# Two-block transformer on one core: the index queries first in the core's filling, the second tile of the selection scored and selected inside the core, and another order between core and attention

## The chip, the cores and the metric

The kernel runs on one core of one Trainium2 chip. The time is device microseconds of one execution. A run of the comparison gives the median of several.

## What is computed

Two blocks work on 512 tokens of width 1024, in fp32. The first (gated linear attention, a convolution, attention in a window, a feed-forward net) is not touched. The second block has two layers. In each one, cut to what matters:

```python
h = rmsnorm_2(x, norm_mix[l]); proj = h @ w_in[l]
aq, ak, av, iq, ik, iw, hq, hf, hi, hg, ga, gb = jnp.split(proj, split_points, axis=-1)
aq, ak = rope(norm(aq)), rope(norm(ak))            # 8 heads of 64
iq, ik = rope(iq), rope(ik)                        # 4 index heads of 64, one key
# selection, per block of 128 queries
rel = relu(einsum('bqhd,bsd->bqhs', iq, ik)); score = einsum('bqh,bqhs->bqs', iw, rel)
_, idx = lax.top_k(where(visible, score, -inf), 128)
y_attn = softmax(q k_sel^T) v_sel
# HGRN core: S_t = diag(f_t) S_{t-1} + k_t v_t^T, o_t = S_t^T q_t, per head of 128
o = rmsnorm_2(o, hgrn_norm[l]) * silu(hg)
merged = sigmoid(ga) * (y_attn @ w_proj_attn[l]) + sigmoid(gb) * (o @ w_proj_hgrn[l])
x = x + merged @ w_out[l]                          # then the feed-forward net
```

The 128 largest scores of a query are found in 16 rounds, each of which takes the eight largest out of the row of scores. The first 128 queries see at most 128 keys and need no rounds, so three query tiles (m = 1, 2, 3, with 256, 384 and 512 scores a row) have 16 rounds each, 48 in a layer.

## The kernel before, in words

Each engine has its own program, written by hand in one order; they meet through semaphores. Every large product is fp32 by three products of split numbers: ScalarE rounds a weight panel (`wh`, line 925, in `ahead`), GpSimd subtracts the rounded part (`wl`, line 909, four pieces of 512 columns), TensorE multiplies (line 458). Weights come in panels of 1 MB in a ring of three slots; SyncE loads the next panel into a slot when the last product of its old panel is done (line 886), and `ahead` rounds it when ScalarE has passed far enough. Results lie in two PSUM pairs that TensorE fills in turn (`new_pair`) and ScalarE or VectorE must free.

A layer of the second block goes through these stages:

- **The core** (`core`, lines 534, 1039, 1508): 8 units, a unit being one tile of 128 tokens and two of the four heads. TensorE sums logarithms (559, 560), ScalarE takes exponentials (1051), VectorE multiplies seven levels of decays (1536), TensorE forms the pair products (580), VectorE copies them under masks (1540, 1550), TensorE makes output and state, VectorE reads both (1555, 1563). Since this is a chain with pauses, a second stream, **the filling** (`side_core_2`, lines 782, 1257, 1906), runs in fixed slots of each unit on all three engines. It has 40 steps, five a unit; on TensorE most are a quarter of a projection (12 matrix instructions of 512 columns, or 24 of 256). `core_steps` places them: one before the second sum, two before the pair products, one before the output, one at the unit's end. The filling projects the index key, the attention queries and keys, then the index queries, the values, and the first half of the output gate (`C_HG`).
- **Between core and attention** (`core_post`, lines 659, 1097, 1633): index scores of tiles 1 and 2 (`index`, `indexed`, `score_keys`), 28 of the 48 rounds (`select`, 1851 and 1853; the result, a bias, 1856), for each half j of the heads the sum of squares (668), the root by logarithm and exponential (1085 to 1095), the gate's arithmetic (`newton` 1628 and 1630, then 1643, 1647), rounding (1112) and the low part (1432). Eight steps of the merge of the first branch run beside it on TensorE.
- **Attention** (lines 673, 1126, 1654): 16 pairs of heads, four for each tile. Index scores of tile 3 come at its head; the remaining rounds and 16 more merge steps go between pairs.

Then the second merge, `w_out` and the feed-forward net follow, nearly all TensorE. For scoring, ScalarE rectifies the products into `tmp3` (line 1123) and VectorE weighs and adds them (1839, 1841); with one buffer, each rectification waits until the scores of the one before are read.

## Time and profile before

| what | us |
| --- | --- |
| median of 3 runs (2764.33 to 2767.23) | 2764.82 |
| the profiled execution's own time | 2762.72 |
| its span | 2760.9 |
| TensorE busy (share of the span) | 2613.3 (95%) |
| VectorE, ScalarE, GpSimd busy | 1161.3, 994.4, 1075.2 |
| core of the first layer, from to | 1037 to 1217.5 |
| between core and attention, from to | 1217.5 to 1279 |
| attention of the first layer, from to | 1279 to 1383 |

Times within the execution count from the span's start. TensorE is busy almost everywhere; the interest lies in the stretches where it is not.

### The profile page before, as it was taken

The numbers are of one execution on the slowest core, as the hardware profiler recorded it, in microseconds if no ns is written. First come the engines' busy times: TensorE is split into PE (matmuls) and PEld (weight loads), VectorE is DVE, ScalarE is ACT, GpSimd is POOL, SyncE is SP. The second block draws the span as 40 slices with busy tenths as digits, with TensorE's granted clock in tenths as the row PEclk, the third lists the DMA queues.
The fourth block names the chain that finished last, engine by engine and source line by source line (L and its number), as shares of the span: only waits on it lengthen the run. The fifth ranks groups of instructions, "written<-read, shape, count | busy, mean of one in ns | idle before, by whom it ended". The sixth has DMA issues, their size and how long they took to land.

```text
span 2760.9 us, 30113 instructions
## 1 busy us (share of the span) xinstructions
PE 2613.3 (95%) x12478; PEld 2125.0 (77%) x12478; DVE 1161.3 (42%) x1928; ACT 994.4 (36%) x1152; POOL 1075.2 (39%) x816
## 2 busy tenths in 40 slices
PE   6999999999999979997999999999998799999999
PEld 4887777887888767875687888888787568788887
DVE  5243343356423455758624211124575862511112
ACT  3423443343323344434424322234443442422220
POOL 3333332544445433212244544544321224354452
PEclk8999999999999999999999999999999899999999
DMA  4222212222232321111122322323111112232322
GB/s 146 68 77 76 77 62 77 92 92 92 92 106 88 96 71 52 46 46 61 31 92 92 105 94 92 107 92 92 46 47 47 61 42 94 88 99 92 102 96 76
DMA packets 206707, 221.05 MB, mean 80 GB/s; under 512 B 3713, under 2 KB 197467, under 8 KB 206443
## 3 DMA queue, kind: packets, MB, share of 16 engines
q1 hardware_dynamic: 206064, 218.97, 24.7%
q8 instruction: 99, 1.62, 0.2%
q14 instruction: 37, 0.30, 0.0%
q10 hardware_dynamic: 507, 0.15, 0.0%
HBM read 217.01 MB, written 2.10 MB: 79 GB/s over the span
## 4 chain that ended last, share of the span: by engine, by line
PE 82%; DVE 12%; ACT 5%; issue 1%; DMA 0%; DVEq 0%; SPq 0%; ACTq 0%
PE psum L458 72%; PE psum L580 2%; ACT wh L925 1%; DVE score L1853 1%; DVE top L1851 1%; PE psum L702 1%; PE psum L690 1%; PE psum L681 1%; DVE ul L1726 1%; DVE ul L1432 1%; DVE dec L1536 1%; PE psum L559 1%; DVE score L1841 1%; PE psum L560 1%; DVE merged L1749 1%
## 5 line engine op out<-in xcount | busy, mean ns | idle before, releaser
L909 POOL TENSOR_TENSOR wl<-raw,wh 128x512 fp32r<-128x512 f32 x812 | 1075.0, 1357 | 1659.8 <-ACT wh L925 1659.7
L458 PE MATMUL psum<-uh,wh 128*128 128x512 f32 x2024 | 812.4, 401 | 25.7 <-DVE ul L1726 4.4
L458 PE MATMUL psum<-ul,wh 128*128 128x512 f32 x2024 | 799.6, 395 | 0.0
L458 PE MATMUL psum<-uh,wl 128*128 128x512 f32 x2024 | 799.1, 395 | 0.0
L925 ACT CAST wh<-raw 128x2048 fp32r<-128x2048 f32 (+1 forms) x206 | 387.1, 1880 | 305.9 <-DMA raw<-in_w_ffn_out 118.0
L458 PEld LDWEIGHTS psum<-uh,wh 128*128 128x128 f32 x2024 | 387.8, 192 | 123.7 <-issue 22.0
L458 PEld LDWEIGHTS psum<-uh,wl 128*128 128x128 f32 x2024 | 386.4, 191 | 83.0
L458 PEld LDWEIGHTS psum<-ul,wh 128*128 128x128 f32 x2024 | 387.1, 191 | 79.2 <-issue 1.0
L458 PE MATMUL psum<-fh,wh 128*128 128x512 f32 x528 | 205.4, 389 | 0.0
L458 PE MATMUL psum<-fl,wh 128*128 128x512 f32 x528 | 205.4, 389 | 0.0
L458 PE MATMUL psum<-fh,wl 128*128 128x512 f32 x528 | 205.4, 389 | 0.0
L1768 DVE TENSOR_TENSOR xT<-xT,psum 128x1024 f32<-128x1024 f32 (+1 forms) x48 | 56.0, 1166 | 293.1 <-PE psum L458 292.8
L1814 DVE TENSOR_TENSOR tmp<-tmp,psum 128x1024 f32<-128x1024 f32 x22 | 26.9, 1221 | 357.5 <-PE psum L458 357.5
L458 PE MATMUL psum<-vh,wh 128*128 128x512 f32 x288 | 116.0, 403 | 10.2 <-DVE xT L1995 8.3
L458 PEld LDWEIGHTS psum<-fl,wh 128*128 128x128 f32 x528 | 99.1, 188 | 20.8
L458 PEld LDWEIGHTS psum<-fh,wl 128*128 128x128 f32 x528 | 99.1, 188 | 20.5
L458 PEld LDWEIGHTS psum<-fh,wh 128*128 128x128 f32 x528 | 99.1, 188 | 20.5
L458 PE MATMUL psum<-vh,wl 128*128 128x512 f32 x288 | 113.2, 393 | 0.0
L458 PE MATMUL psum<-wh,uh 128*128 128x256 f32 x320 | 94.2, 294 | 12.1 <-DVE ul L1432 12.1
L458 PE MATMUL psum<-vl,wh 128*128 128x512 f32 x256 | 99.7, 389 | 0.0
L458 PE MATMUL psum<-wl,uh 128*128 128x256 f32 x320 | 91.7, 286 | 0.0
L458 PE MATMUL psum<-wh,ul 128*128 128x256 f32 x320 | 91.6, 286 | 0.0
(318 smaller groups left out, 3276.1 us busy)
## 6 DMA issues: line engine op xcount, KB each, us to landing
raw<-in_w_in SPq DMA_DIRECT2D x78, 1024.0 KB, 5.2
raw<-in_w_ffn_in SPq DMA_DIRECT2D x44, 1024.0 KB, 5.1
raw<-in_w_up SPq DMA_DIRECT2D x22, 1024.0 KB, 5.1
raw<-in_w_ffn_out SPq DMA_DIRECT2D x16, 1024.0 KB, 5.1
raw<-in_w_down SPq DMA_DIRECT2D x8, 1024.0 KB, 5.0
raw<-in_w_out SPq DMA_DIRECT2D x8, 1024.0 KB, 5.1
raw<-in_w_ffn_out SPq DMA_DIRECT2D x8, 768.0 KB, 4.4
raw<-in_w_o SPq DMA_DIRECT2D x4, 1024.0 KB, 5.0
```

The source lines that it names most:

```text
L458: ins = mm(dst, x, y, start=first and i == 0, stop=last and i == len(todo) - 1)
L559: mm(X[1 + b][:, 0:3 * P], lth[:, u % 2, i, :], summask[:, cols], start=True, stop=False)
L560: ins = mm(X[1 + b][:, 0:3 * P], ltl[:, u % 2, i, :], summask[:, cols], start=False, stop=True)
L580: ins = mm(level_scores(l)[:, i, :, :], dec[:, i, l, :], odd_blocks(dec[:, i, l, :], l), start=True, stop=True)
L681: ins = mm(X[e][:, 0:(b1 - b0) * P], q[HD * e:HD * (e + 1), p, m * P:(m + 1) * P], kof(2 * p + e)[:, b0 * P:b1 * P], start=True, stop=True)
L690: ins = nc.tensor.transpose(X[2][:, b * P:(b + 1) * P], prob[i % 2][:, e, b * P:(b + 1) * P], ident)
L702: ins = mm(X[3][HD * e:HD * (e + 1), 0:P], vof(2 * p + e, b), probT[:, e, (b - b0) * P:(b - b0 + 1) * P], start=(b == b0), stop=(b == b1 - 1))
L909: ins = nc.gpsimd.tensor_tensor(wl[p % 3][:, w], raw[p % 3][:, w], wh[p % 3][:, w].bitcast(F32), ALU.subtract)
L925: nc.scalar.copy(wh[p % 3][:, 0:nk * width], raw[p % 3][:, 0:nk * width]).then_inc(S.hi_done, 1)
L1432: v.tensor_tensor(dst, src, high.bitcast(F32), ALU.subtract).then_inc(sem, 1)
L1536: ins = v.tensor_tensor(e[:, :, :, part, :], e[:, :, :, part, :], x[:, :, :, part, :], ALU.mult)
L1768: v.tensor_tensor(x, x, src, ALU.add).then_inc(pair_free[(n.q - 1) % 2], 1)
```

## The change

In words, for each of the two layers:

- The index queries (`C_IQ`) are projected second in the filling, before the attention queries; ScalarE and no longer VectorE copies them out and scales `iw`. The key's and queries' rotation comes in unit 1. The four norm-and-rotate groups of the attention queries and keys each move one unit later.
- Tile 1 is scored in unit 6 (step 31 of the filling, counted from 0), and its 16 rounds run inside the core: eight at the end of unit 6, eight at the end of unit 7.
- The second half of the output gate (`C_HG + 256`) is a panel of its own right behind the first, no longer between the merge's gates.
- Between core and attention stands `indexed_post`. The squares of the first half are taken before the core ends. Tile 2 is scored between the two halves of the gate, from two buffers (`rectified`), and nine of its rounds follow. Seven rounds of tile 2 and 16 of tile 3 are left for the attention (23, before 20). The merge steps stand two and six around the second sum, before four and four.
- TensorE goes on to the attention's first products when ScalarE has read the sums (`g_mean`), not when the root is done.
- `score1`, `bias1` and the second silu have places of their own, and tile 3 is rectified into two buffers.

The three `indexed_post` in the diff are TensorE's, ScalarE's and VectorE's, in this order; the piece with `index(1)` is from TensorE's filling, the last two pieces are from VectorE's.

```diff
-                  C_IK, C_AQ, C_AQ + 256, C_AK, C_AK + 256, C_IQ, C_AV, C_AV + 256, C_HG):
+                  C_IK, C_IQ, C_AQ, C_AQ + 256, C_AK, C_AK + 256, C_AV, C_AV + 256, C_HG, C_HG + 256):
...
-        merge(w, C_G2 + D, a["w_proj_hgrn_2"][l], C_HG + 256)
+        merge(w, C_G2 + D, a["w_proj_hgrn_2"][l])
...
-SIDE_POST_2 = (4, 4)
+SIDE_POST_2 = (2, 6)
...
-SELECT_EARLY = 14
+SELECT_CORE, SELECT_POST = (8, 8), 9
...
+            def indexed_post(side, side_steps):
+                sum_heads()
+                finish(project(uh, ul))
+                index(2)
+                take_on(side, side_steps[0])
+                sum_heads()
+                take_on(side, side_steps[1])
+                pe.wait_ge(S.g_mean, t.up(S.g_mean, 2))
...
                 yield from project_tokens()
-                pe.wait_ge(pair_free[queries % 2], queries // 2 + 1)
-                turn(iq, rot)
+                index(1)
                 yield
...
+            def indexed_post(side, side_steps):
+                root_heads()
                 act.wait_ge(S.i_scored, t.up(S.i_scored))
+                inverse_root(tmp[2][:]).then_inc(S.g_root, 1)
+                silu_gate(silu1[:])
+                rectify(2, 0)
+                high_branch(0)
+                rectify(2, 1)
+                act.wait_ge(S.out_read, t.up(S.out_read))
+                square_heads(1)
+                take_on(side, side_steps[0])
+                root_heads()
+                act.wait_ge(S.g_split, t.up(S.g_split))
+                inverse_root(tmp[2][:]).then_inc(S.g_root, 1)
+                take_on(side, side_steps[1] - 2)
+                high_branch(1)
+                take_on(side, 2)
...
+            def rectify(m, j):
+                src = next_pair()
+                act.wait_ge(S.pair_full, n.q)
+                fn(index_tiles(m)[j], src[:, :, 0:(m + 1) * P], ACT.Relu).then_inc(pair_free[(n.q - 1) % 2], 1)
+                ahead()
...
+            def indexed_post(g, side, side_steps, selection):
+                gate_heads(0, g, True, tmp[0][:])
+                next_pair()
+                score_keys(2)
+                take_on(selection, SELECT_POST)
+                take_on(side, side_steps[0])
+                gate_heads(1, g, True, silu1[:])
+                take_on(side, side_steps[1])
...
+                score_keys(1)
                 yield
                 yield from wait_steps(2)
-                cosine(iq[:])
+                take_on(selection, SELECT_CORE[0])
                 yield
                 yield from passed(1)
...
+                yield from wait_steps(3)
+                next_pair()
+                take_on(selection, SELECT_CORE[1])
                 yield
```

VectorE at the end of the core (line 1563 writes the last state) and behind it, in the kernel before; `score_80` and `score_81` are the scores of tiles 1 and 2:

```order
L1563 SCALAR_TENSOR_TENSOR state<-state,small,psum 128x128 x2
L2140 TENSOR_SCALAR hidden<-const 128x128
L1839 TENSOR_SCALAR score_80<-tmp,iw 128x256
L1841 SCALAR_TENSOR_TENSOR score_80<-tmp,iw,score_80 128x256 x3
L1844 TENSOR_TENSOR score_80<-score_80,const 128x128
L1839 TENSOR_SCALAR score_81<-tmp,iw 128x384
L1841 SCALAR_TENSOR_TENSOR score_81<-tmp,iw,score_81 128x384 x3
L1844 TENSOR_TENSOR score_81<-score_81,const 128x128
L1851 MAX top<-score_80 128x8
L1853 MATCH_REPLACE score_80<-top,score_80 128x256
...
L1628 TENSOR_TENSOR tmp<-tmp 128x1024
```

And now, from the scoring in unit 6 to the first product of the gate:

```order
L1897 TENSOR_SCALAR score_80<-tmp,iw 128x256
L1899 SCALAR_TENSOR_TENSOR score_80<-tmp,iw,score_80 128x256 x3
L1902 TENSOR_TENSOR score_80<-score_80,const 128x128
...
L1618 SCALAR_TENSOR_TENSOR state<-state,small,psum 128x128 x2
L1909 MAX top<-score_80 128x8
L1911 MATCH_REPLACE score_80<-top,score_80 128x256
...
L1579 COPY small<-dec 128x2
...
L1914 TENSOR_SCALAR bias_85<-score_80 128x256
L2205 TENSOR_SCALAR hidden<-const 128x128
L1683 TENSOR_TENSOR tmp<-tmp 128x1024
L1685 SCALAR_TENSOR_TENSOR tmp<-tmp 128x1024
```

Scoring and the first eight rounds stand in unit 6, ahead of the last unit's first operation (1579); the next eight and the bias behind the last state; nothing of tile 1 stands between core and gate any more.

ScalarE behind the core, in the kernel before (`tmp<-gq` is the square of the core's output, `early` a gate of the merge):

```order
L1300 ACTIVATE tmp<-psum 128x1024
L925 CAST wh<-raw 128x2048
L1123 ACTIVATE tmp<-psum 128x2x256 x2
L1123 ACTIVATE tmp<-psum 128x2x384 x2
L1101 ACTIVATE tmp<-gq 128x1024
L1085 ACTIVATE tmp<-psum,small 128x1024
L1088 ACT_TABLE_LOAD
L1088 ACTIVATE tmp<-tmp 128x1024
L1093 ACT_TABLE_LOAD
L1093 ACTIVATE tmp<-tmp 128x1024
L1095 ACTIVATE tmp<-tmp 128x1024
L1112 CAST brh_52<-tmp 128x1024
```

And now, from the first root's last operation on:

```order
L1114 ACTIVATE tmp<-tmp 128x1024
L1119 ACT_TABLE_LOAD
L1119 ACTIVATE silu_88<-psum 128x1024
L944 CAST wh<-raw 128x2048
L1147 ACTIVATE rectified_86<-psum 128x2x384
L944 CAST wh<-raw 128x2048
L1127 CAST brh_52<-tmp 128x1024
L1147 ACTIVATE rectified_87<-psum 128x2x384
L1123 ACTIVATE tmp<-gq 128x1024
```

The rounding of the first half (1127, before 1112) now stands behind the second silu and two weight panels (944).

## Rows read from the trace of the kernel before

**Rows 1.** Stretches: start:end, length; busy PE, PEld, DVE, ACT, POOL; clock, DMA share, GB/s.
```profile
1037.00:1217.50 180.50, 175.23 (x1015) 150.36 (x1015) 109.15 (x265) 73.79 (x73) 46.52 (x35) 0.98 0.16 47
1217.50:1279.00 61.50, 46.54 (x172) 33.14 (x172) 49.50 (x108) 32.82 (x30) 15.36 (x12) 0.85 0.22 69
1279.00:1383.00 104.00, 92.62 (x517) 63.94 (x517) 75.25 (x183) 43.46 (x106) 25.13 (x20) 0.92 0.12 37
2112.00:2173.50 61.50, 45.24 (x172) 32.75 (x172) 49.54 (x108) 32.81 (x30) 15.36 (x12) 0.88 0.22 69
```

**Rows 2.** The chain that ended last, cut to 1218 to 1383: shares by line.
```profile
by line: PE psum L458 24.2%; DVE score L1853 11.1%; DVE top L1851 10.1%; PE psum L702 6.4%; PE psum L690 6.1%; DVE score L1841 5.1%; PE psum L681 5.0%; ACT wh L925 3.2%; issue 3.0%; ACT tmp L1123 2.9%; DVE tmp L1643 1.7%; DVE score L1839 1.
```

**Rows 3.** ScalarE from the core's end: start, length, line, operation, idle before it.
```profile
1217.50 1.28 ACT L1300 ACT_TABLE_LOAD   x1 [10.09 <-PE psum L458]
...
1219.72 1.89 ACT L925 CAST wh<-raw 128x2048 fp32r<-128x2048 f32 x1
...
1238.30 1.12 ACT L1085 ACTIVATE tmp<-psum,small 128x1024 f32<-128x1024 f32 x1 [5.60 <-PE psum L668]
...
1244.20 1.06 ACT L1095 ACTIVATE tmp<-tmp 128x1024 f32<-128x1024 f32 x1
...
1276.50 1.04 ACT L1112 CAST brh<-tmp 128x1024 fp32r<-128x1024 f32 x1 [9.83 <-DVE tmp L1647]
```

**Rows 4.** VectorE, 1228 to 1272: scoring, rounds, the gate's first product.
```profile
1228.26 0.42 DVE L1839 TENSOR_SCALAR score<-tmp,iw 128x384 f32<-128x384 f32 x1 [0.62 <-ACT tmp L1123]
...
1230.34 1.27 DVE L1841 SCALAR_TENSOR_TENSOR score<-tmp,iw,score 128x384 f32<-128x384 f32 x2 [1.01 <-ACT tmp L1123]
...
1253.38 0.43 DVE L1851 MAX8 top<-score 128x8 f32<-128x256 f32 x1
...
1254.37 0.43 DVE L1851 MAX8 top<-score 128x8 f32<-128x256 f32 x1
...
1256.27 0.56 DVE L1851 MAX8 top<-score 128x8 f32<-128x384 f32 x1
...
1257.52 0.56 DVE L1851 MAX8 top<-score 128x8 f32<-128x384 f32 x1
...
1271.27 1.23 DVE L1628 TENSOR_TENSOR tmp<-tmp 128x1024 f32<-128x1024 f32 x1
```

**Rows 5.** GpSimd: the low parts of weight panels.
```profile
1065.71 10.48 POOL L909 TENSOR_TENSOR wl<-raw,wh 128x512 fp32r<-128x512 f32 x8 [13.22 <-ACT wh L925]
1099.62 5.01 POOL L909 TENSOR_TENSOR wl<-raw,wh 128x512 fp32r<-128x512 f32 x4 [23.42 <-ACT wh L925]
...
1254.81 10.09 POOL L909 TENSOR_TENSOR wl<-raw,wh 128x512 fp32r<-128x512 f32 x8 [27.79 <-ACT wh L925]
```

**Rows 6.** TensorE steps in the chain: start, length, line, matrix instructions.
```profile
1176.05 2.87 PE psum L458 x24
...
1214.69 2.75 PE psum L458 x12
...
1291.44 4.54 PE psum L458 x12
```

**Rows 7.** TensorE: one sum over the squares of two heads.
```profile
1236.38 1.88 PE L668 MATMUL psum<-tmp,ones 128*128 128x512 f32 x4
```

**Rows 8.** VectorE (two) and ScalarE (one) in the core's units 6 and 7.
```profile
1186.62 2.07 DVE L1970 TENSOR_TENSOR iq<-iq,tmp 128x1024 f32<-128x1024 f32 x1
...
1202.57 0.17 DVE L1524 COPY small<-dec 128x2 f32<-128x2 f32 x1 [8.45 <-ACT dec L1051]
...
1184.36 1.90 ACT L925 CAST wh<-raw 128x2048 fp32r<-128x2048 f32 x1 [2.95 <-DMA raw<-in_w_in]
```

**Rows 9.** VectorE: one level product of the core's unit 1 and one of unit 2.
```profile
1072.45 1.35 DVE L1536 TENSOR_TENSOR dec<-dec,gq 128x128 f32<-128x128 f32 x1
...
1099.29 0.29 DVE L1536 TENSOR_TENSOR dec<-dec,gq 128x128 f32<-128x128 f32 x1
```

**Rows 10.** ScalarE at the first pair of heads: the second rectification.
```profile
1286.11 1.03 ACT L1123 ACTIVATE tmp<-psum 128x1024 f32<-128x1024 f32 x1 [3.06 <-DVE score L1841]
```

More of the change, by code:

```diff
@@ L115, in __init__ @@
         self.pair_scaled = sem("pair_scaled")
+        self.g_mean = sem("g_mean")
         self.alpha_done = sem("alpha_done")
@@ L340, in build_program, with index_tiles @@
         gaT = at("gaT", 63, [RANK, T])
+        def index_tiles(m):
+            if m == 1:
+                return [tmp[3][:].rearrange("p a (b t) -> p (a b) t", b=2)[:, 2 * j:2 * j + 2, :] for j in range(2)]
+            return [(rectified[0] if m == 2 else tmp[3])[:, :, 0:(m + 1) * P], rectified[1][:, :, 0:(m + 1) * P]]
         sq = at("sq", 49, [P, MC, T])
@@ L359, in build_program @@
         inverse = at("inverse", 48.5, [P, P])
-        bias1 = at("bias1", 44, [P, 2 * P])
+        bias1 = nc.alloc_sbuf_tensor_at("bias1", [P, 2 * P], F32, offset=walpha_at + 4 * 2 * P)
+        rectified = [at(f"rectified{i}", 32 + 4 * i, [P, 2, T]) for i in range(2)]
+        silu1 = at("silu1", 12, [P, 2, T])
         bias2 = at("bias2", 42, [P, 3 * P])
@@ L784, in side_core_2 @@
                 yield from project(uh, ul, (0,))
-                keys = n.q - 1
+                yield from project(uh, ul)
+                queries = n.q - 1
+                dst = new_pair()
+                mm(dst[:, 0, :], rot, ik[:], start=True, stop=True)
+                for m in range(NT):
+                    ins = nc.tensor.transpose(dst[:, 1, 4 * m:4 * m + 4], iwT[:, m * P:(m + 1) * P], ident[HD:HD + 4, HD:HD + 4])
+                ins.then_inc(S.pair_full, 1)
+                pe.wait_ge(pair_free[queries % 2], queries // 2 + 1)
+                turn(iq, rot)
+                yield
                 for j in range(4):
@@ L796, in side_core_2 @@
                     yield
-                yield from project(uh, ul)
-                queries = n.q - 1
-                dst = new_pair()
-                pe.wait_ge(pair_free[keys % 2], keys // 2 + 1)
-                for m in range(NT):
-                    nc.tensor.transpose(dst[:, 1, 4 * m:4 * m + 4], iwT[:, m * P:(m + 1) * P], ident[HD:HD + 4, HD:HD + 4])
-                mm(dst[:, 0, :], rot, ik[:], start=True, stop=True).then_inc(S.pair_full, 1)
-                yield
                 yield from project_tokens()
-                pe.wait_ge(pair_free[queries % 2], queries // 2 + 1)
-                turn(iq, rot)
+                index(1)
                 yield
@@ L1279, in side_core_2 @@
                 yield from passed(2)
+                yield from evict(iq[:])
+                src = next_pair()
+                act.wait_ge(S.pair_full, n.q)
+                fn(tmp[1][:, 0, :], src[:, 0, :], ACT.Copy)
+                fn(iw[:].rearrange("p m h -> p (m h)"), src[:, 1, 0:4 * NT], ACT.Copy,
+                   scale=1.0 / 16).then_inc(pair_free[(n.q - 1) % 2], 1)
+                ahead()
+                next_pair()
+                ahead()
+                yield
                 for j in range(4):
@@ new lines, in gate_heads @@
+            def gate_heads(j, g, same, gate):
+                dve.wait_ge(S.g_root, t.up(S.g_root))
+                newton(tmp[1][:], tmp[2][:])
+                for i in range(2):
+                    col = g if same else g + 2 * j + i
+                    ins = v.scalar_tensor_tensor(tmp[3][:, i, :], gq[:, 2 * j + i, :], vech[:, col:col + 1],
+                                                 tmp[3][:, i, :], ALU.mult, ALU.mult)
+                ins.then_inc(S.dve_chain, 1)
+                dve.wait_ge(S.dve_chain, t.up(S.dve_chain))
+                v.tensor_tensor(tmp[3][:], tmp[3][:], gate, ALU.mult).then_inc(S.g_prod, 1)
+                dve.wait_ge(S.g_prod, t.up(S.g_prod))
+                dve.wait_ge(S.b_hi, t.up(S.b_hi))
+                low(brl[0][:, 2 * j:2 * j + 2, :], tmp[3][:], brh[0][:, 2 * j:2 * j + 2, :],
+                    S.branch_ready if j else S.g_split)
@@ L2137, in _ @@
                     dve.wait_ge(S.dve_chain, t.up(S.dve_chain))
-                core(1.0, side_core_2(l), SIDE_CORE_2)
+                selection = select_all()
+                core(1.0, side_core_2(l, selection), SIDE_CORE_2)
                 side = merge(early, first=True)
```

174 lines of the change are left out of this document (77 added, 97 removed).

## The prediction

> **What bounds it now.** The page says that TensorE is almost always busy, so a gain can only come out of its pauses. I looked for them with the table of stretches. The core of the first layer keeps TensorE busy for 175.2 of 180.5 us; between core and attention it is 46.5 of 61.5, part of that at a granted clock of 0.85, and in attention 92.6 of 104 [rows 1]. The second layer's stretch between core and attention is as long [rows 1], so every term below counts twice. The chain of waits, cut to the stage, says who sets the pace: besides TensorE's products its largest shares are VectorE's rounds (L1853, L1851), 21%, then scoring L1841 [rows 2]. Between core and attention VectorE is the bound: it is busy 49.5 of 61.5 us [rows 1] and nearly all the rest is a hand-over with ScalarE. At the end of the core it is the other way round: before unit 7 VectorE stands idle for 8.45 us [rows 8]. The change moves VectorE's work from the one place to the other.
>
> I count from t = 0 at 1217.5, where TensorE's last step of the core has ended [rows 6] and ScalarE starts the silu of the gate [rows 3]. The stage ends with the gate's product of the second half of the heads, for which ScalarE's rounding L1112 waits until 1276.50 [rows 3]: t = 59.0. From there on attention follows in nearly the same order before and after.
>
> **The new path from t = 0 to that product.** The durations are those of the rows.
>
> - ScalarE: table and silu, until the cast of a panel begins, 2.2; cast until 4.1; first root, from the start of L1085 to the end of L1095 7.0 [rows 3]. The squares were made before the core's end and TensorE's sum takes 1.9 [rows 7], which is hidden. The root is ready at 11.1. VectorE's product (from L1628's start to the waiting copy) takes 5.2 [rows 3, 4]: 16.3. VectorE's eight rounds behind the last state end near t = 6.5 and hold nobody.
> - TensorE: sum 1.9, then the second gate projection, four steps of 2.75 [rows 6]: 12.9. ScalarE: table and silu 2.2, cast 1.9: 17.0. It rectifies half of tile 2, 0.8 for 768 of the 1024 columns that take 1.03 [rows 10]: 17.8. Then a second cast is ahead of the rounding. Its panel may be loaded only from 12.9 on; in unit 6 a step ended at 1178.92 and the cast of the panel so released began at 1184.36 [rows 6, 8], 5.4 later. So: begin at 18.4, end at 20.3, rounding 1.0 [rows 3]: 21.3. VectorE, done at 16.3, waits five microseconds for this.
> - VectorE: low part 1.2, scoring of tile 2 0.42 + about 0.65 + 1.27 + 0.3 [rows 4], together 3.9. But GpSimd splits the two panels from 17 to 27 (5.0 a panel [rows 5]), and an instruction of VectorE with two SBUF inputs is held up when it starts in the middle of that: the same 1024 columns take 2.07 in L1970 and 1.23 in L1628 [rows 8, 4], a level product 1.35 against 0.29 [rows 9]. Four instructions at about 0.9 more: ready at 28.7. Nine rounds of 384 at 1.25 (the distance of two maxima [rows 4]): 40.0. I take the rounds as not held up, since those from 1256.27 on keep the distance while GpSimd works on the two panels that it began at 1254.81 [rows 4, 5]. The product of the second half, 5.2: **t = 45.2, a gain of 13.8**.
> - TensorE has in that time 1.9 + 11 + 8 steps of 2.75 + 1.9, near 38 us with index products, so it isn't the bound; the second root (7.0 from about 25) is ready before 40.
>
> **Inside the core.**
>
> - Unit 6, step 31. Removed are the rotation of the index queries: 1.23 and, held up by GpSimd, 2.07 [rows 8]. Added is the scoring of tile 1, 0.4 + 3 x 0.6 + 0.3, but its second half waits for a rectification that stands behind the cast at 1184.36 to 1186.3 [rows 8], and the three instructions then meet GpSimd. The masks begin near 1190.9 and no longer at 1188.7: **2.2 lost**. Bounds: 0 if nothing is held up, 5 if all seven of scoring's and rounding's instructions are.
> - The normalization that moves into unit 6 stood in four of the other units up to now, in a core that keeps TensorE busy for 175.2 of 180.5 us [rows 1]; I cost it at nothing, since the slot is the same and the exponential behind it comes as late there.
> - The eight rounds of 0.98 [rows 4] at the end of unit 6, 7.9, go into the idle 8.45 [rows 8]. I cost them at nothing; the cover is thin, 0.6 us, and anything beyond lengthens the core one for one. Bounds 0 and 7.9; I take the lower end because the idle row is the very place.
> - Unit 1: the index queries' rotation comes here. In unit 1 GpSimd splits two panels in one go, 10.5 us, and the level products start into it, at 1.35 each [rows 5, 9]. That stays, with ScalarE about 1 us earlier: **1.0 gained**. The copies that ScalarE takes over are as long as VectorE's and lie in its idle time.
>
> **Attention.** 23 rounds instead of 20 fall on 11 pairs, one more each at pairs 0, 5 and 10. At pair 0 VectorE is the bound: **1.25 lost**. At the other two the pace is nearly even: **0.8 lost** of 2.9 (bounds 0 and 2.9). The second rectification of tile 3 waited 3.06 us for its buffer [rows 10] and now has its own; VectorE gets back about **1.2**, the rectification's 1.03 and a hand-over.
>
> **Sum.** Per layer -13.8 + 2.2 - 1.0 + 1.25 + 0.8 - 1.2 = -11.75, for two layers -23.5. The profiled execution took 2762.7 ; it lies 2.1 below the median of 2764.8. So 2739.2 against the former, **2741** against the latter.
>
> The Trainium skill ("ScalarE: Activation LUTs", What ACT_TABLE_LOAD costs) states 2.66 us for each switch of tables, 1.28 of load and 1.38 of drain. By that, the path to 21.3 would be some 0.8 longer and the sum -22. The trace shows 1.28, and the cast 2.2 after the load's start leaves no room for a drain behind it [rows 3], so the sum goes by the trace.
>
> **The rivals.**
>
> 1. *VectorE is freed fully.* If ScalarE's second panel cast is early and GpSimd's pieces fall beside the scoring, the stage falls by about 17 and unit 6 loses nothing: -17.5 a layer, **2730**. For it: GpSimd's panels and VectorE's bursts often miss each other, as in unit 2 with 0.29 [rows 9]. Against it: both casts stand in the order right ahead of the rounding. Chance 0.15.
> 2. *TensorE's clock takes half.* The new path leaves TensorE pauses at t = 13 to 18 and 42 to 57. A step at the lower clock takes 4.54 and not 2.75 [rows 6], and in attention the clock is 0.92 now [rows 1]. Three or four more such steps where TensorE leads cost 6 a layer: **2753**. Chance 0.12.
> 3. *The rounds in the core are exposed.* Unit 6 is late by the scoring (3.5 beyond the 2.2) and the eight rounds then lie before the level products: 7.9. That eats the 11.75: **2765**, no change. Chance 0.06.
> 4. *Slower: collisions in units 2 to 5.* There the level products end just before GpSimd starts on its panel: the last of unit 2 at 1099.58, the panel at 1099.62 [rows 5, 9]. If the shifted projections let a panel start 3 to 4 us sooner than the products, each unit has four products waiting for a piece of GpSimd, near 1.05 each: 4.2. All four units in both layers give +33.6: **2775**. It decides against the change from the sixth unit hit of eight on. Against it: in these units the cast waits for the load of its panel, and that comes from the same step as now. Chance 0.05. The Trainium skill ("SBUF — State Buffer", SBUF: two separate sides) says that the port VectorE and GpSimd share is locked for a whole instruction and the loser waits; that is what the two lengths of a level product show here.
>
> **How the numbers follow.** My case has 0.62, with its own range from the bounds: 2735 (nothing held up in unit 6) to 2749 (5 in unit 6, 2.9 in attention, one more held-up chain). Rivals 1 and 2 are faster too. A measurement of this kernel tells about 0.2%, 5.5 us, from no change, that is below 2759 or above 2770. Faster 0.87 (the first three cases, less 0.02 for the end of rival 2's), within 0.2% 0.07, slower 0.06. The range, 2729 to 2757, takes in my case and most of rivals 1 and 2, and leaves out 3 and 4 and the tails.
>
> **What would show it.** Right: the core still ends within 2 or 3 us of where it did, counted from its start; the product of the second half comes 44 to 48 us after that; attention lasts 103 to 105; in the chain cut to the stage the rounds' share falls from 21% to about 15%; the rounding of the first half waits for nobody but comes behind two casts. Wrong: level products of 1.3 us in units 2 to 5 (rival 4), an idle VectorE before unit 7 gone and the unit longer (rival 3), steps of 4.5 us in attention (rival 2), a second product before t = 42 (rival 1). If the core changes its length outside units 1 and 6, the count is wrong there.

## The result, and the profile after

The changed kernel takes **2751.9 us** (median of four runs, 2748.07 to 2755.41), the kernel before 2765.4 on the same chip (four runs): a ratio of 0.995, 95% interval 0.9933 to 0.9967. In a later series it took 2749.2 (five runs, 2746.4 to 2750.38), ratio 0.9941 (0.9928 to 0.9953). All nine runs have a median of 2749.5; experiments are set against that number below, since the kernel before had medians of 2764.0 to 2764.3 in the three series of experiments. It is faster, by 13 to 15 us, and the forecast was 23.5. The profiled execution took 2752.76, its span is 2751.0 against 2760.9. 2751.9 lies inside the stated range of 2729 to 2757, but not in the range of the forecast's own case, 2735 to 2749, and nearer to rival 2's 2753 than to the 2741 of the sum: some 5 us a layer are missing, and below they are looked for term by term.

The page's first lines, and the table of stretches of the changed kernel. The stretches are the core of the first layer, the stage between core and attention, attention, and that stage in the second layer.

```profile
span 2751.0 us, 30103 instructions
PE 2609.2 (95%) x12478; PEld 2123.0 (77%) x12478; DVE 1175.1 (43%) x1924; ACT 996.1 (36%) x1158; POOL 1078.3 (39%) x816
```
```profile
1037.00:1224.00 187.00, 180.16 (x1021) 154.19 (x1020) 120.71 (x298) 78.86 (x81) 45.65 (x34) 0.95 0.15 46
1224.00:1271.00 47.00, 38.77 (x164) 28.91 (x162) 36.95 (x64) 28.83 (x26) 16.54 (x12) 0.98 0.29 90
1271.00:1376.60 105.60, 92.71 (x517) 62.78 (x517) 81.64 (x193) 43.24 (x106) 26.53 (x20) 0.93 0.12 36
2115.00:2162.50 47.50, 38.71 (x164) 28.92 (x162) 37.42 (x67) 29.33 (x26) 16.55 (x12) 0.98 0.28 89
```

Set against [rows 1]: the stage fell from 61.5 to 47.0, as forecast, but the core grew from 180.5 to 187.0 and attention from 104.0 to 105.6. The core's growth is not even over its eight units. The next table is worked out from VectorE's updates of the state, one at each unit's end (L1559 and L1563 before, L1614 and L1618 after); unit 0 is counted from VectorE's copy of the decay (L1524, L1579). "First attention" is the distance from the last state to VectorE's first masked logits.

```
us                     unit 0  unit 1  2 to 4 each  unit 5  unit 6  unit 7  first attention
before, layer 1         11.98   30.61        22.0    20.06   21.34   21.21     64.18
before, layer 2         12.00   30.51        22.1    20.08   21.33   21.22     64.18
after, layer 1          11.99   30.60        22.0    22.30   23.66   22.40     50.01
after, layer 2          15.65   30.47        22.1    22.29   23.55   22.34     50.01
after, second profile:
  layer 1               11.99   30.53        22.0    22.29   23.04   21.22     49.98
  layer 2               11.98   30.61        22.1    22.29   22.99   21.22     49.97
```

So a layer loses 2.2 in unit 5, 1.7 to 2.3 in unit 6, nothing or 1.2 in unit 7, and in unit 0 of one layer 3.65. It gains 14.2 behind the core and loses some 1.4 in attention. With a start 0.7 later, the first layer comes to -6.3 (from 1382.90 to 1376.58 at attention's end), the second to -3.6: together the 9.9 of the spans. The start itself says nothing about the change: the first layer's core begins at 1043.40 before and at 1044.11 after, and anywhere from 1043.1 to 1047.1 in the fourteen profiles of this document, with the same program ahead of it.

**Behind the core.** ScalarE, then VectorE; columns are start, length, engine, line, operation, and in brackets the idle time before it.

```profile
1236.56 1.03 ACT L1119 ACTIVATE silu<-psum 128x1024 f32<-128x1024 f32 x1 [1.66 <-PE psum L468]
1237.48 1.89 ACT L944 CAST wh<-raw 128x2048 fp32r<-128x2048 f32 x1
1239.27 0.81 ACT L1147 ACTIVATE rectified<-psum 128x768 f32<-128x768 f32 x1
1241.61 1.91 ACT L944 CAST wh<-raw 128x2048 fp32r<-128x2048 f32 x1 [1.53 <-DMA raw<-in_w_proj_hgrn]
1243.42 1.04 ACT L1127 CAST brh<-tmp 128x1024 fp32r<-128x1024 f32 x1
...
1268.78 1.04 ACT L1127 CAST brh<-tmp 128x1024 fp32r<-128x1024 f32 x1 [12.71 <-DVE tmp L1697]
```
```profile
1244.57 2.25 DVE L1487 TENSOR_TENSOR brl<-tmp,brh 128x1024 fp32r<-128x1024 f32 x1 [5.67 <-ACT brh L1127]
1246.85 1.30 DVE L1897 TENSOR_SCALAR score<-rectified,iw 128x384 f32<-128x384 f32 x1
1248.19 3.76 DVE L1899 SCALAR_TENSOR_TENSOR score<-rectified,iw,score 128x384 f32<-128x384 f32 x3
```
```profile
1239.44 11.44 POOL L928 TENSOR_TENSOR wl<-raw,wh 128x512 fp32r<-128x512 f32 x8 [7.53 <-ACT wh L944]
```

The sum is the forecast's nearly to the microsecond. The first half's rounding stands behind two casts and ends at 1244.4, t = 20.6 from the core's end at 1223.9 (forecast 21.3); VectorE idles 5.67 for it (forecast "five"); GpSimd's two panels cover low part and scoring, of which five instructions and not four are held up, by 3.7 us together where 3.6 were forecast (the additions take 1.25 each); the second half's product reaches ScalarE at 1268.78, t = 44.9 (forecast 45.2). The last row answers to the last of [rows 3]. One piece went another way: the forecast had a table load in front of each silu, and the trace has the second one made at 1233.62, before the 1.66 of idle shown above. The product of the first half was ready at t = 15.0 and not 16.3. This changed nothing, since the rounding hung on the second panel, whose cast began at 17.7 (forecast 18.4).

**In units 5 and 6.** TensorE before the change (unit 5), then after it (unit 5, and the row at which unit 6 waits):

```profile
1159.80 0.40 PE L802 MATMUL psum<-const,iwT 4*128 4x4 f32 x4
1160.14 1.12 PE L803 MATMUL psum<-ik,const 128*128 128x512 f32 x2
```
```profile
1160.53 1.96 PE L822 MATMUL psum<-qksq,const 128*128 128x512 f32 x4
1162.32 1.88 PE L800 MATMUL psum<-ak,const 128*128 128x512 f32 x4
...
1183.07 1.13 PE L752 MATMUL psum<-ik,iq 64*128 64x256 f32 x8
...
1196.79 0.49 PE L600 MATMUL psum<-attT,gv 128*128 128x128 f32 x2 [2.03 <-DVE attT L1605]
```

Unit 5 now holds the means and the rotation of the last normalization, 3.8 us of TensorE, where the index keys' small rotation with 1.5 stood. No run moves the normalization alone; that it costs the 2.2 is read from these rows (3.8 less 1.5, in a unit in which TensorE is busy throughout). In unit 6 TensorE waits 2.03 us for the masks, which VectorE copies behind the scoring of tile 1:

```profile
1188.69 0.48 DVE L1899 SCALAR_TENSOR_TENSOR score<-tmp,iw,score 128x256 f32<-128x256 f32 x1
1189.92 2.44 DVE L1899 SCALAR_TENSOR_TENSOR score<-tmp,iw,score 128x256 f32<-128x256 f32 x2 [0.75 <-ACT tmp L1147]
1192.39 1.27 DVE L1902 TENSOR_TENSOR score<-score,const 128x128 f32<-128x128 f32 x1
...
1194.17 2.56 DVE L1605 COPY_PREDICATED attT<-pairmask,psum 128x128 f32<-128x128 uint8 x7
...
1209.02 0.17 DVE L1579 COPY small<-dec 128x2 f32<-128x2 f32 x1 [1.77 <-ACT dec L1070]
```

The last row answers to the 8.45 of [rows 8]: with the eight rounds ahead of it VectorE still idles 1.77 before unit 7, and 0.58 in the second profile, whose unit 6 is shorter.

### The profile page after: what moved, and what is told of

The parts are those of the page before. It is cut to its first block, busy times and chain, and to the rows that moved or that the text cites. A ratio compares the mean times of both kernels' runs of the same rounds, so it can differ in the third digit from the quotient of the medians.

```text
span 2751.0 us, 30103 instructions
## 1 busy us (share of the span) xinstructions
PE 2609.2 (95%) x12478; PEld 2123.0 (77%) x12478; DVE 1175.1 (43%) x1924; ACT 996.1 (36%) x1158; POOL 1078.3 (39%) x816
## 4 chain that ended last, share of the span: by engine, by line
PE 80%; DVE 13%; ACT 4%; DMA 1%; issue 1%; DVEq 0%; SPq 0%; ACTq 0%
PE psum L468 71%; ACT wh L944 2%; PE psum L590 2%; DVE score L1911 1%; DVE top L1909 1%; DVE score L1899 1%; PE psum L723 1%; DVE ul L1790 1%; DVE dec L1591 1%; PE psum L711 1%; DVE ul L1487 1%; PE psum L569 1%; DVE tmp L1736 1%; DVE merged L1813 1%; DVE normed L1548 1%
## 5 line engine op out<-in xcount | busy, mean ns | idle before, releaser
L468 PEld LDWEIGHTS psum<-fh,wl 128*128 128x128 f32 x528 | 99.1, 188 | 20.6
L468 PEld LDWEIGHTS psum<-fh,wh 128*128 128x128 f32 x528 | 99.1, 188 | 20.6
```

The lines of the kernel that those rows point to most:

```text
L468: ins = mm(dst, x, y, start=first and i == 0, stop=last and i == len(todo) - 1)
```

## The experiments

In the diffs, `rectify(m, j, False)` and `silu_gate(dst, False)` leave out the `ahead()` behind the activation, that is, the cast of the next panel, which is made at the next `ahead()`. `ahead(done=1)` counts one more pair of results as finished, so that both panels that wait there are cast at once.

### 1. Casts away from the level products of units 0 and 1

```diff
@@ ScalarE, side_core_2, the changed kernel @@
-                yield from passed(2)
-                yield from evict(iq[:])
+                yield
+                next_pair()
+                yield
+                yield
+                ahead(done=1)
+                yield
+                yield
+                src = next_pair()
+                act.wait_ge(S.pair_full, n.q)
+                fn(iq[:], src, ACT.Copy).then_inc(pair_free[(n.q - 1) % 2], 1)
+                ahead()
+                yield
```

> On the changed kernel: ScalarE's two casts of panels that stand before the level products of units 0 and 1 are moved behind the copy of unit 0's transposed keys, so that GpSimd splits both of them beside the masks of unit 0; unit 1 then has one panel and not two. Nothing else is moved. Theory A (GpSimd's panels hold up VectorE's level products in unit 1, TensorE is bound there by it, and which of the two wins in unit 0 differs from layer to layer): level products of 0.29 in unit 0 of both layers and mostly in unit 1, unit 1 shorter by 5 to 8 us, unit 0 of the second layer by 3.6: 12 to 20 us in all, about 2736. Theory B (unit 1 is bound by TensorE's own products): less than 4 us gained.

The same in the kernel before the change, whose first group of projections is a normalization:

```diff
@@ ScalarE, side_core_2, the kernel before @@
-                yield from passed(2)
+                yield
+                next_pair()
+                yield
                 for j in range(4):
-                    yield from wait_steps(3)
+                    yield
+                    if j == 0:
+                        ahead(done=1)
+                    yield from wait_steps(2)
```

> The same displacement of casts in the kernel before the change, whose unit 1 still holds a normalization (its means and rotation are 3.6 us of TensorE). Theory A (the changed kernel lost 2.2 us in unit 5 to the normalization that came there, and got nothing back in unit 1 only since GpSimd binds that unit): unit 1 gets shorter here too, but stays 2 us longer than in the changed kernel with displaced casts, so that the two differ by 2 to 4 us more for two layers than before and after do, 15.5 to 17.5 instead of 13.5. Theory B (the place of the normalization is indifferent): they differ by 13.5 as before.

Measured: on the changed kernel **2727.5** (2724.03 to 2730.42; ratio to before 0.987, 0.9856 to 0.9883), 22 below the changed kernel; on the kernel before 2746.3 (ratio 0.9939, 0.9925 to 0.9952), 17.8 below it. Rows of the first of the two kernels, GpSimd and a level product of unit 1:

```profile
1053.80 10.01 POOL L928 TENSOR_TENSOR wl<-raw,wh 128x512 fp32r<-128x512 f32 x8 [10.61 <-ACT wh L944]
1072.66 4.99 POOL L928 TENSOR_TENSOR wl<-raw,wh 128x512 fp32r<-128x512 f32 x4 [8.85 <-ACT wh L944]
```
```profile
1068.87 0.29 DVE L1601 TENSOR_TENSOR dec<-dec,gq 128x128 f32<-128x128 f32 x1
```

No level product of any unit is held up in either kernel, and unit 1 takes 21.15 (changed) and 21.6 (before) where it took 30.6. Theory A holds, with more gained than it said: 9.4 us in each layer were the price of seven held-up products out of 16 and of what follows from the late levels. The kernel before had this loss too, and the change left it alone.

Not all of it is waiting. Behind the pair products TensorE has twelve instructions of a projection. Their stretch before the change, after it, and nearly the whole of unit 1 with the casts moved; the columns are those of [rows 1], the clock the third figure from the end, and the count takes in one instruction at each edge:

```profile
1080.90:1084.90 4.00, 4.00 (x14) 3.25 (x14) 1.38 (x4) 0.00 (x0) 0.00 (x0) 0.68 0.00 0
```
```profile
1080.65:1085.60 4.95, 4.95 (x14) 3.92 (x14) 1.39 (x4) 0.00 (x0) 0.00 (x0) 0.54 0.00 0
```
```profile
1054.00:1079.00 25.00, 25.00 (x138) 20.69 (x138) 11.56 (x37) 8.18 (x9) 14.80 (x12) 1.00 0.14 43
```

TensorE waits up to 1.9 us at a time for the late levels, and behind that it is granted the lower of its two levels (1.2 and not 2.4 GHz) for 6.9 us in the kernel before and for 10.2 in every unit 1 of the changed kernel. The twelve take 4.0 and 4.95 us; with the casts moved, at a clock of 1.00, they take 2.85. So of the 9.4 us 7.3 lie ahead of the end of the pair products and 2.1 are the clock behind them.

The second expectation failed in both its numbers. The two unit 1s differ by 0.45, not 2: what the normalization left behind in unit 1 was at once filled by the index queries' rotation (1.98, and 1.4 for the keys, against 3.8). And the medians of the two kernels differ by 18.8, more than the 15.5 to 17.5 of theory A and than theory B's 13.5; unit 1 accounts for 0.9 of that, and no run shows the rest. So the 2.2 of unit 5 is no exchange that a hidden stall swallowed: only 0.45 comes back in unit 1 and 0.3 in unit 6 (section 3).

### 2. Chance in unit 0

```diff
@@ ScalarE, side_core_2, against the first kernel of section 1 @@
-                ahead(done=1)
+                ahead()
```

With this only unit 0's panel moves. Beside it the changed kernel ran once more, unedited.

> The changed kernel itself once more, for the spread of its runs and a second profile. In the profiles so far the four last level products of unit 0 are either all held up by GpSimd (unit of 15.65 us) or none of them (12.0), in one of the two layers or in neither, with the same program around them. Theory A (this is left to chance in every run, and is the spread): single runs lie apart by up to 7.3 us, median between 2748 and 2754. Theory B (it is set by the program): all runs within 3 us.

> On the changed kernel: only the cast of the panel that GpSimd splits during unit 0's level products is moved behind unit 0's key copy; the two panels of unit 1 stay where they are. Theory A (chance in unit 0): unit 0 takes 12.0 in both layers, unit 1 its 30.5, runs lie apart by under 4 us, the median 1 to 6 below that of changed_again. Theory B (the spread has another source): the same spread as changed_again, median within 1.

Measured: 2749.2 (2746.4 to 2750.38) and 2747.6 (2746.73 to 2749.34). The first is between the theories: its runs lie 4 us apart and its profile has no held-up product in unit 0. Part of such a spread has nothing to do with unit 0, as the core's start between 1043.1 and 1047.1 shows. The second behaves as theory A has it, 12.0 in both layers and a spread of 2.6, but its median is only 1.6 lower, which these runs hardly tell from nothing. What the profiles do show is the event. Of the 18 layers profiled with the cast in its old place (the kernel before, the changed one twice, and the six of sections 3 to 6), seven had exactly four held-up products (the fifth to the eighth or the sixth to the ninth of 16, not the last four) and a unit 0 of 15.65 to 15.68; eleven had none and 11.97 to 12.00. In the second layer of the changed kernel, VectorE and GpSimd:

```profile
1933.83 0.28 DVE L1591 TENSOR_TENSOR dec<-dec,gq 128x128 f32<-128x128 f32 x1
1934.03 1.38 DVE L1591 TENSOR_TENSOR dec<-dec,gk 128x128 f32<-128x128 f32 x1
```
```profile
1933.78 5.33 POOL L928 TENSOR_TENSOR wl<-raw,wh 128x512 fp32r<-128x512 f32 x4 [5.86 <-ACT wh L944]
```

GpSimd started 0.76 behind the first of the 14 products of this line. In the first layer of the same execution it started at the same distance, and there the products took 0.28 each and its panel 7.44:

```profile
1046.23 7.44 POOL L928 TENSOR_TENSOR wl<-raw,wh 128x512 fp32r<-128x512 f32 x4 [6.88 <-ACT wh L944]
```

### 3. Unit 6: the masks behind the scoring

```diff
@@ ScalarE, side_core_2 @@
-                rectify(1, 0)
+                rectify(1, 0, False)
                 rectify(1, 1)
```

> On the changed kernel: in unit 6 ScalarE rectifies both halves of tile 1's index products before the cast of the next panel, and no longer one before and one behind it. Theory A (the cast between them delays VectorE's scoring into GpSimd's panel, and that is the 2.3 us by which unit 6 is longer than before): VectorE has no idle before the second half's scoring, the scaled additions take near 1.3 for two and not 2.44, unit 6 falls from 23.6 to about 22, 2 to 3 us in all. Theory B (unit 6 waits for the panel, whose transfer ends at the same time, and for the rounds' place): unit 6 stays above 23 and nothing is gained.

```diff
@@ VectorE, side_core_2, the changed kernel @@
-SELECT_CORE, SELECT_POST = (8, 8), 9
+SELECT_CORE, SELECT_POST = (6, 10), 9
...
-                score_keys(1)
                 yield
                 yield from wait_steps(2)
+                score_keys(1)
                 take_on(selection, SELECT_CORE[0])
```

> On the changed kernel: in unit 6 VectorE scores tile 1 behind the unit's state and ahead of the rounds, no longer ahead of the masks; and two of the eight rounds go from there to the end of the core. Theory A (TensorE waits about 1.8 to 2.0 for the masks that stand behind scoring, which is most of what unit 6 grew by): the wait ahead of unit 6's output products is gone, unit 6 is 21.3 to 21.8, unit 7 at most 0.5 longer, 3 to 5 us in all. Theory B (unit 6 grew because TensorE has more to do, its index products of 1.13): unit 6 stays above 22.5, under 2 us gained.

Measured: 2749.3 for the first (2746.08 to 2751.09), which is no difference. The idle is gone, but scoring still meets GpSimd's panel: in the second layer the three additions take 2.41, TensorE waits only 0.79 and unit 6 is 22.07, as theory A said; in the first they take 3.39, TensorE waits 1.77, its clock falls and unit 6 is 23.64. **2740.6** for the second (2738.38 to 2746.68; ratio 0.9909, 0.9894 to 0.9924), 9 below the changed kernel, twice what was expected; its unit 6 takes 21.02 in both layers. TensorE has no wait there, and the additions are free of GpSimd:

```profile
1196.08 0.39 PE L600 MATMUL psum<-attT,gv 128*128 128x128 f32 x2
```
```profile
1198.65 1.53 DVE L1899 SCALAR_TENSOR_TENSOR score<-tmp,iw,score 128x256 f32<-128x256 f32 x3
```

So theory A of the second holds: unit 6 is long because masks stand behind scoring. TensorE alone would now need less there than before the change (21.02 against 21.34), since the index products replaced the queries' rotation; that 0.3 of unit 5's 2.2 is given back once the wait is gone. Of the 9 us the trace explains 4 in unit 6 (23.0 to 21.0, twice), and up to 3.6 more by the clock: in the changed kernel's first profile TensorE ran at a lower clock behind its 2.03 of waiting (1.86 in the second layer), in the second profile, behind 1.76 and 1.71, it did not. Stretches around the end of unit 6, first and second profile:

```profile
1196.80:1204.00 7.20, 7.20 (x45) 7.20 (x46) 5.30 (x18) 0.13 (x1) 0.00 (x0) 0.76 0.01 3
```
```profile
1195.50:1203.00 7.50, 5.74 (x47) 5.53 (x46) 5.77 (x19) 0.00 (x0) 0.26 (x1) 1.00 0.01 3
```

A mean of 0.76 is a mixture of the two levels, 1.2 and 2.4 GHz. It costs 0.6 in unit 6 and 1.2 in unit 7 (22.40 against 21.22) of each layer. The length of the wait alone doesn't decide it. Over all fourteen profiles 19 layers have a wait of 1.67 to 2.03 there, and in nine of them the clock fell, at a price of 1.5 to 1.9 for units 6 and 7 together; the kernel with all casts moved (section 7) waits 1.83 in both layers of one execution, and the clock fell in the second alone (unit 6 of 24.02 against 23.11). In the nine layers that wait at most 0.79 it never fell. Nine of 19, at 1.7 each, are some 1.6 us for two layers; the rest of the 9 stays open.

### 4. The rounds in the core

```diff
-SELECT_CORE, SELECT_POST = (8, 8), 9
+SELECT_CORE, SELECT_POST = (0, 8), 17
```

> The eight rounds of tile 1 at the end of unit 6 are moved behind the core, to the nine behind the scoring of tile 2 (none in unit 6, still eight behind the last state, 17 behind the scoring). Theory A (the rounds in the core cost nothing, their time came out of VectorE's idle 8.45): the core keeps its length, the gate's product of the second half comes 7.9 later in each layer (eight rounds of 0.98), the whole 13 to 16 us slower than the changed kernel, at about 2767. Theory B (the core grew because of the rounds): the core gets shorter by some of the 6.4 us by which it grew, and the whole is only 3 to 6 us slower.

Measured: **2763.4** (11 runs, 2758.36 to 2768.07; ratio 0.9999, 0.999 to 1.0007), 14 above the changed kernel. First attention comes 58.2 after the last state, not 50.0; unit 7 takes 21.22 in the first layer, exactly as in the changed kernel's second profile with the rounds (22.55 in the second layer, behind a fallen clock). Theory A: the eight rounds in unit 6 cost nothing and save 8.2 us in each layer. Of all that the change does they are worth most, 8.2 of the 14.2 that the stage lost (how the other 6.0 divide among the earlier squares, the second buffers, the moved gate panel and the order of the merge steps, no run tells): put back behind the core, they leave a kernel that isn't measurably faster than the one before.

### 5. ScalarE's order behind the core

```diff
@@ ScalarE, indexed_post @@
-                rectify(2, 0)
+                rectify(2, 0, False)
                 high_branch(0)
```

> On the changed kernel: behind the core ScalarE rounds the first half's gated product before the second panel's cast and no longer after it. Theory A (the first half's rounding is late by the cast and its DMA, and VectorE idles 5.7 us for it): the rounding ends near 1241 and not 1244.4, the idle of VectorE's low part falls to some 2.3, the second half's product comes 3 to 4 us sooner, 6 to 8 us in all, about 2745. Theory B (GpSimd's two panels hold up the scoring behind it, so that it ends at the same time): under 2 us.

```diff
@@ ScalarE, indexed_post @@
-                silu_gate(silu1[:])
-                rectify(2, 0)
+                silu_gate(silu1[:], False)
+                rectify(2, 0, False)
                 high_branch(0)
-                rectify(2, 1)
+                rectify(2, 1, False)
                 act.wait_ge(S.out_read, t.up(S.out_read))
                 square_heads(1)
+                ahead()
```

> On the changed kernel: behind the core both casts of panels that now lie between silu, rectifications and rounding are made behind the squares of the second half, so that ScalarE serves VectorE first and GpSimd's two panels fall beside VectorE's rounds. Theory A (VectorE is the bound behind the core, and two things hold it up: the wait for the first rounding, and GpSimd's panels beside the scoring): low part of the first half at once and in 1.23, scaled additions near 0.64 each, the second half's product 6 to 7 us sooner than in the changed kernel in each layer, attention not longer; 12 to 14 us in all, about 2738. It also prices rival 1 of the prediction. Theory B (the panels come too late for TensorE's merge steps, or meet scoring and rounds anyway): under 4 us.

Measured: 2744.6 (2740.41 to 2750.06; ratio 0.9934, 0.9922 to 0.9947) and **2736.3** (2730.52 to 2739.77; ratio 0.9896, 0.9881 to 0.9912). With the rounding first, the low part ends 3.8 sooner against the last state, but scoring meets GpSimd throughout, and attention starts only 1.9 sooner: between the theories. With both casts late it starts 42.76 behind the last state and not 50.0, 7.2 sooner in each layer, as theory A said. VectorE and GpSimd in that kernel:

```profile
1241.29 1.23 DVE L1490 TENSOR_TENSOR brl<-tmp,brh 128x1024 fp32r<-128x1024 f32 x1 [1.18 <-ACT brh L1128]
1242.55 0.42 DVE L1900 TENSOR_SCALAR score<-rectified,iw 128x384 f32<-128x384 f32 x1
1243.01 1.93 DVE L1902 SCALAR_TENSOR_TENSOR score<-rectified,iw,score 128x384 f32<-128x384 f32 x3
```
```profile
1244.72 10.18 POOL L928 TENSOR_TENSOR wl<-raw,wh 128x512 fp32r<-128x512 f32 x8 [11.59 <-ACT wh L944]
```

The additions cost 0.64 each and not 1.25, the idle is 1.18 and not 5.67, and GpSimd works beside the rounds.

### 6. Attention's beginning

```diff
@@ ScalarE, attention @@
-                    rectify(NT - 1, 0)
-                    rectify(NT - 1, 1)
+                    rectify(NT - 1, 0, False)
+                    rectify(NT - 1, 1, False)
```

> On the changed kernel: at the start of attention ScalarE makes no cast behind the two rectifications of tile 3, as it was before the change. Theory A (the cast between them sends GpSimd into VectorE's scoring, which is why attention grew by 1.4 where 0.85 was forecast): scaled additions of tile 3 shorter, attention 1 to 1.5 shorter in each layer, 2 to 3 us in all. Theory B (the growth is only the three more rounds, 1.25 at pair 0 and under that at two others): no difference.

Measured: 2744.1 (2742.39 to 2750.39; ratio 0.9927, 0.9914 to 0.9941), 5 below where 2 to 3 were expected. From first to last masked logits it is 90.66 and 90.15 us in the two layers, against 92.34 and 92.30 in the changed kernel (92.97 in its second profile) and 90.94 before the change. The last two additions of tile 3, in the changed kernel and in this one:

```profile
1278.36 3.34 DVE L1899 SCALAR_TENSOR_TENSOR score<-rectified,iw,score 128x512 f32<-128x512 f32 x2
```
```profile
1284.10 1.54 DVE L1900 SCALAR_TENSOR_TENSOR score<-rectified,iw,score 128x512 f32<-128x512 f32 x2
```

Theory A: the cast cost about 2 us in each layer. Attention's length varies by itself from profile to profile, so all of them count here: 91.1 to 93.0 in the 18 layers of the changed order with the cast, 89.2 to 90.7 in the six without it. The old order has 90.9 twice, and 89.8 and 92.4 in section 1's kernel; that the new one without the cast is shorter than the old isn't shown.

### 7. Together

> The four displacements together (casts of units 0 and 1 behind unit 0's key copy, both rectifications first in unit 6, casts behind the squares behind the core, none between tile 3's rectifications). Theory A (their gains add, since they lie in different stretches of one chain): 24 of the first, 2 of the second, 13 of the third and 2 of the fourth below the changed kernel, at about 2710 to 2715. Theory B (VectorE's relief only hands the bound to TensorE and its clock): 2722 or more.

> all_casts_moved together with score_behind_state. If unit 6's wait is real there too: 3 to 5 us below all_casts_moved, about 2701. If the rounds behind the scoring then reach into unit 7: no gain, or up to 2 us lost.

Measured: **2705.0** (2700.23 to 2709.25; ratio 0.9785, 0.9769 to 0.98) and **2702.8** (2699.76 to 2705.66; ratio 0.9775, 0.9762 to 0.9788). The first is 44.5 below the changed kernel; the four by themselves gave 22.0, 0.2, 13.2 and 5.4, together 40.8, so the parts add. The granted clock over the whole execution, 0.976 in the changed kernel, is 0.984 here. The second takes unit 6 to 21.02 in both layers (23.11 and 24.02 in the first kernel, where TensorE waits 1.83); medians of two series only 2.2 apart, with overlapping intervals, don't show that as a gain of the whole (3 to 5 were expected). Both beat both kernels, by 44 to 47 and by 59 to 61 us, with as many instructions as the changed kernel (30103).

## Why the prediction was right or wrong

- **The stage behind the core: right.** The product of the second half came at t = 44.9 (forecast 45.2), by the reasons given: two casts ahead of the rounding, 5.67 of idle, held-up instructions behind it (five, not four), rounds not held up. One sign was wrong. The rounds' share of the chain was to fall from 21% to about 15%; here it is in the same cut, which is not the stage alone but reaches from the core's end to attention's end:

```profile
by line: PE psum L468 19.8%; DVE score L1911 12.1%; DVE top L1909 11.2%; DVE score L1899 5.5%; DVE tmp L1736 5.0%; DVE inverse L1755 4.4%; PE psum L723 4.3%; PE psum L711 3.5%; ACT wh L944 3.5%; DMA raw<-in_w_proj_hgrn 3.2%; issue 2.8%; PE 
```

  It is 23%, against 21% in [rows 2]. The cut mixes two things. In the stage alone the rounds' share fell from 48% to 23%. In attention alone it rose from 5.4% to 24.7%: most of attention's chain now runs through VectorE, and I had counted rounds on the path only where the change put them.
- **The rounds in the core, cost 0: right,** and the thin cover of 0.6 held. Experiment 4 shows it.
- **Normalization moved into the later units, "I cost it at nothing, since the slot is the same": wrong, 2.2 in each layer.** The prediction has it moving into unit 6; counted from 0 as elsewhere it is unit 5 that gets the fourth one. The slot is the same, its content not: 3.8 us of TensorE took the place of 1.5, in a unit that TensorE fills. I looked at whose exponential comes late and did not add TensorE's instructions per unit, though [rows 1] said that the core is TensorE's.
- **Unit 6, 2.2 lost: right in size and in kind,** scoring that is held up ahead of the masks. It is 1.7 at the full clock and 2.3 behind a fallen one. What I had not priced is this clock behind TensorE's wait: 0.6 there and 1.2 in unit 7, when it falls. That is rival 2's mechanism, in the core and not in attention.
- **Unit 1, 1.0 gained: wrong, nothing.** The first half of the step came true. GpSimd's two panels start 21.4 us behind the core's start (1065.51 less 1044.11) and no longer 22.3 (1065.71 in [rows 5], less 1043.40), and the level products come 0.9 sooner with them. What ate the gain is TensorE's clock: it stays at the lower level for 10.2 and not 6.9 us, and the twelve products behind the pair products take 4.95 and not 4.0. Gain and loss are as good as equal (30.60 and 30.61). Experiment 1 shows what bound the unit, and that it was worth 9.4 and not 1.0.
- **Attention, 0.85 lost: 1.4 to 2.0.** The cast that `rectify` now makes between tile 3's halves was overlooked; it costs 2 (experiment 6). So the three rounds, less what the second buffer gives back, cost less than was put down for them; by how much, the variation between profiles doesn't let one say.
- **Rival 1** ("VectorE freed fully", 17.5 a layer, 2730) did not happen by itself. Made to happen in experiment 5, the way from the last state to first attention shrinks by 21.4 us (64.18 to 42.76), more than the 17 that it was priced at, and the kernel takes 2736.3 and not 2730, since the core keeps its losses. **Rival 4** had the right mechanism in the wrong unit: units 2 to 5 have no collision in any profile, unit 0 has one by chance, +3.65 in one layer of the first profile. **Rival 3** didn't happen: unit 6 is longer by what the scoring costs, and the rounds fit.

In sum for the first layer: -11.75 forecast; 2.2 (unit 5), 1.0 (unit 1), 0.1 and 1.2 (units 6 and 7), 0.5 (attention), 0.7 (a later start of the core, within what the start varies anyway) and -0.4 (the stage) make -6.4, and -6.3 was measured. So the forecast was right about the stage, which gives the whole gain, and its wide range covered the rest; three terms of the core and attention (unit 5, unit 1, the overlooked cast) were wrong, all in the direction of too much gain, and the clock added to them. The sign "the core still ends within 2 or 3 us of where it did" (it took 5.7 longer) and the last one, a core that changes outside units 1 and 6, both said so. One part of the account stays read and not tested, the 2.2 of unit 5.

## What to carry to other kernels

When a change permutes pieces of filling work among slots of a loop, add up the bounding engine's instructions slot by slot; "the same slot" says nothing. When two engines hold each other up, look at what triggers the one off the critical path: moving the casts that start GpSimd, with no work removed, was worth three times the change itself (44.5 against 14.8 us), what TensorE's clock gave back included. A wait that looks worth 2 us can cost up to as much again in TensorE's clock behind it. And put what another engine waits for (the masks) ahead of what nobody waits for yet (the scoring), also inside one engine's idle time.

## What the runs showed of the hardware

Who wins between VectorE and GpSimd isn't settled by the program. With GpSimd starting 0.76 us behind the first of a row of 0.2-us-spaced products, its panel took 7.44 and VectorE lost nothing, or the panel took 5.33 and four of the next products 1.35 to 1.38 each, in the two layers of one execution; once VectorE had lost, it lost four times in a row, once for each of the panel's four instructions. In the Trainium skill ("SBUF — State Buffer", SBUF: two separate sides) whoever starts first holds the shared port for the whole instruction, in a lock against operations with two SBUF inputs or in a 2-port mode. The trace agrees in size: beside the panel a level product takes 1.35 where it takes 0.28 alone, and the difference of 1.07 is most of the 1.3 that one of GpSimd's instructions takes. Operations with one SBUF input are held up here too (whether by that mode, no run tells):

```profile
1229.70 1.07 DVE L1914 TENSOR_SCALAR bias<-score 128x256 f32<-128x256 f32 x1
...
1299.10 0.36 DVE L1914 TENSOR_SCALAR bias<-score 128x384 f32<-128x384 f32 x1
```

The first, of 256 columns, runs beside GpSimd's panel of 1226.81 to 1231.9, the second, of 384, beside none. The search for maxima is not held up: the eight rounds ahead of the first row keep their distance of 0.98 through that panel's start.

TensorE's granted clock fell behind some waits of 1.67 to 2.03 us in a core that is otherwise full and not behind others of the same length (nine of 19), and behind none of at most 0.79 (none of nine). With identical code this makes 1.5 to 1.9 us of difference for a layer.
